# A hybrid decoder layer in fp32r: NSA's q projected first by token tile, 64-column narrow and compressed-score matmuls, and a later chain for the compressed scores

## What is computed

```python
def reference(x, attn_norm_g, w_in, ...):
    h = x
    for l in range(DEPTH):                                   # DEPTH = 1
        a = rms_norm(h, attn_norm_g[l])
        (nq, nkv, ngate, dq, dk, dv, fq, fk, fv, ff, mg) = jnp.split(a @ w_in[l], split_points, axis=-1)
        qa = rms_norm(nq.reshape(B, S, NSA_HEADS, hd), nsa_q_g[l]) * scale
        kv = nkv.reshape(B, S, 3, 2, NSA_GROUPS, hd)
        k_cmp = rms_norm(compress(kv[:, :, 0, 0], ...), nsa_k_g[l, 0])
        v_cmp = compress(kv[:, :, 0, 1], ...)
        ...
        o_a = nsa_attention(qa, k_cmp, v_cmp, k_slc, ..., k_win, ..., ngate..., cmp_end)
        ...                                                  # diff_attention, forgetting_attention
        gates = jax.nn.sigmoid(mg.reshape(B, S, N_BRANCH, D))
        merged = (gates[:, :, 0] * (o_a @ w_br[l, 0]) + gates[:, :, 1] * (o_b @ w_br[l, 1])
                  + gates[:, :, 2] * (o_c @ w_br[l, 2]))
        h = h + merged @ w_o[l]
        h = h + conv_ffn(rms_norm(h, ffn_norm_g[l]), ...)
    return h

# in nsa_attention, for 128 tokens at a time:
dist_c = tpos[:, None] - cmp_end[None, :]
s_c = jnp.einsum('btgrd,bngd->bgrtn', qg, k_cmp)             # 8 heads, 31 compressed keys
s_c = s_c - sl[..., None] * dist_c
p_c = masked_softmax(s_c, dist_c >= 0)
o_c = jnp.einsum('bgrtn,bngd->btgrd', p_c, v_cmp)
```

## Time and profile before

| | us |
|---|---|
| median of 3 runs | 976.08 (975.51 to 976.84) |
| profiled execution, device time | 978.79 |
| its span, first to last instruction | 977.0 |
| PE busy in the span | 958.5 (98%) |
| DVE, ACT, POOL busy | 559.8, 426.2, 209.8 |
| PE's start in the span, first transpose | 8.25 |

### The profile page before, as it was taken

The page is one execution under the profiler, slowest core; times in us unless marked ns, Lnnn a source line. Parts: engine busy times, 40 slices in busy tenths (PEclk is TensorE's granted clock), DMA queues, the critical chain, the costliest instruction groups (busy, mean ns, idle before and its releaser), DMA issues.

```text
span 977.0 us, 12185 instructions
## 1 busy us (share of the span) xinstructions
PE 958.5 (98%) x4625; PEld 794.5 (81%) x4625; DVE 559.8 (57%) x1063; ACT 426.2 (44%) x770; POOL 209.8 (21%) x250
## 2 busy tenths in 40 slices
PE   6999999999999999999999999999999999999998
PEld 5787877788888888888888888888888888888887
DVE  6737787864366895546567454655655665522113
ACT  5335776754256653445777333423222322221110
POOL 3000457640001112212455220121112121100000
PEclk9999999999999999999999999999999999999999
DMA  6512110112222212222211242223222322232222
GB/s 237 219 44 86 45 44 1 43 45 86 87 89 85 87 44 87 86 87 87 81 50 44 87 172 87 87 89 123 91 87 87 121 95 86 87 117 99 87 87 86
DMA packets 13691, 86.33 MB, mean 88 GB/s; under 512 B 1473, under 2 KB 1985, under 8 KB 4289
## 3 DMA queue, kind: packets, MB, share of 16 engines
q1 hardware_dynamic: 13632, 85.55, 24.2%
HBM read 83.44 MB, written 2.10 MB: 88 GB/s over the span
## 4 chain that ended last, share of the span: by engine, by line
PE 89%; DVE 7%; ACT 2%; issue 2%; DMA 0%; SPq 0%; ACTq 0%; DVEq 0%
PE ps L1531 22%; PE ps L1533 22%; PE ps L1532 22%; PE ps L1715 10%; PE ps L1559 4%; PE ps L1672 1%; PE ps L1671 1%; PE ps L1700 1%; DVE prob_n L1232 1%; DVE wl L1013 1%; PE ps L1586 1%; DVE ptn_l L1267 1%; PE ps L1793 1%; PE ps L1795 1%; DVE prob L1232 1%
## 5 line engine op out<-in xcount | busy, mean ns | idle before, releaser
L1013 DVE TENSOR_TENSOR wl<-raw,wh 128x512 fp32r<-128x512 f32 (+2 forms) x118 | 173.5, 1475 | 136.4 <-ACT wh L701 133.8
L701 ACT ACTIVATE wh<-raw 128x2048 fp32r<-128x2048 f32 (+1 forms) x58 | 109.4, 1886 | 157.9 <-PE ps L1533 140.3
L1531 PE MATMUL ps<-aT_h,wh 128*128 128x512 f32 (+1 forms) x376 | 146.7, 390 | 0.8 <-DVE aT_l L1022 0.8
L1532 PE MATMUL ps<-aT_l,wh 128*128 128x512 f32 (+1 forms) x376 | 146.4, 389 | 0.0
L1533 PE MATMUL ps<-aT_h,wl 128*128 128x512 f32 (+1 forms) x376 | 146.4, 389 | 0.0
L1531 PE MATMUL ps<-wh,aT_h 128*128 128x512 f32 x256 | 102.0, 398 | 0.0
L1533 PE MATMUL ps<-wh,aT_l 128*128 128x512 f32 x256 | 100.0, 391 | 0.0
L1532 PE MATMUL ps<-wl,aT_h 128*128 128x512 f32 x256 | 99.8, 390 | 0.0
L1514 POOL TENSOR_TENSOR gl<-gl,rstdT 128x512 f32<-128x512 f32 x22 | 44.5, 2022 | 234.5 <-ACT gl L987 234.5
L1470 POOL TENSOR_SCALAR prob_n<-prob_n,coef 128x384 f32<-128x384 f32 (+3 forms) x64 | 67.7, 1071 | 114.6 <-DVE coef L1249 114.3
L1531 PEld LDWEIGHTS ps<-aT_h,wh 128*128 128x128 f32 (+1 forms) x376 | 70.0, 186 | 16.5 <-issue 1.0
(11 more groups left out here) (250 smaller groups left out, 1796.1 us busy)
## 6 DMA issues: line engine op xcount, KB each, us to landing
raw<-wblk SPq DMA_DIRECT2D x72, 1024.0 KB, 4.7
x<-x SPq DMA_DIRECT2D x4, 512.0 KB, 5.2
w_sb<-w SPq DMA_DIRECT2D x1, 2048.0 KB, 9.2
hid<-x SPq DMA_DIRECT2D x1, 2048.0 KB, 7.7
out<-outt SPq DMA_DIRECT2D x8, 256.0 KB, 2.0
stage<-consts SPq DMA_DIRECT2D x1, 708.5 KB, 4.7
later<-consts SPq DMA_DIRECT2D x1, 448.0 KB, 5.4
par<-params SPq DMA_DIRECT2D x1, 204.5 KB, 8.3
```

The lines of the kernel that those rows point to most:

```text
L701: nc.scalar.activation(wh[b % 2][:, 0:n], raw[b % RING][:, 0:n], ACT.Copy).then_inc(hi_ready, 4)
L1013: ins = nc.vector.tensor_tensor(wl[b % RING][:, cols], raw[b % RING][:, cols], wh[b % 2][:, cols].bitcast(f32), ALU.subtract)
L1531: nc.tensor.matmul(dst, a_h, b_h, start=start, stop=False)
L1532: nc.tensor.matmul(dst, a_h, b_l, start=False, stop=False)
```

## The change

- The block order of NSA becomes `nq`, `small`, `cmp`, `sw`. `nq0` is loaded in four pieces between the tiles of `x`; a row `grow` of the norm's gains is loaded too.
- The gain goes onto `x` ahead of the transpose: two matmuls spread `grow` over 128 partitions into two PSUM banks, and DVE's scaling multiplies by the row factor and by that bank. A transposed tile (four chunks of one token tile, a half of the channels) is taken by ACT and DVE tile by tile. Eight transposes of the identity run on PE ahead of all.
- `first_tiles` projects `nq0` for token tiles 0 to 3 as each is ready, then `nq1`; the next tile's transposes stand between a tile's sixth and seventh matmul.
- `small` holds the high and the low weights side by side as 64 stationary columns: 16 matmuls for 24. `ST` adds the two halves with a stacked identity `id2`.
- The steps after the projections are in another order: the DVE and ACT work of the `nq` chunks and of `gate0`'s block stands ahead of `compression(1)` and `(2)`, and PE's `compression(0)`, `(1)`, `(2)` stand later.
- `SC` is 8 matmuls of 64 columns (high and low keys side by side) with no distance matmul. DVE adds the distance and the two halves, then takes minimum and subtracts (`SCV`); POOL multiplies by the slopes (`SCM`) and, after `CN`, by the coefficients (`CNM`); ACT's exponential is `SCA`.
- In the table `SC` stands at 4 and `TC` at 12, the steps between at 5, 6, 7, 8, 9; `OC` for both groups at 15. `SC` and `ON(i, 0)` use bank 2, `TC` and `ON(i, 1)` bank 3. `ON(i, 0)` is opened by `VA`.

```diff
-PROJ = {NSA: ["cmp", "small", "nq", "sw"], DIFF: ["dq", "dk", "dv"], FOX: ["fq", "fk", "fv"]}
+PROJ = {NSA: ["nq", "small", "cmp", "sw"], DIFF: ["dq", "dk", "dv"], FOX: ["fq", "fk", "fv"]}
...
-            put(per * i + 3, "SC", i)
-            put(per * i + 5, "CN", i)
-            put(per * i + 7, "TC", i)
+
+            put(per * i + 4, "SC", i)
...
+            put(per * i + 12, "TC", i)
...
+            sp.dma_start(x0[:, 0, :], xv[0]).then_inc(x_in[0], 16)
+            sp.dma_start(grow[:, :].rearrange("o (p c) -> o p c", c=KD), params[:, C_ROW:C_ROW + KD].rearrange("(o p) c -> o p c", o=1)).then_inc(grow_in, 16)
+            first(0)
+            first(1)
+            sp.dma_start(x0[:, 1, :], xv[1]).then_inc(x_in[1], 16)
...
+            def x_scale(n):
+
+                half, t = divmod(n, TT)
+                dve.wait_ge(rstd_ready, t + 1)
+                dve.wait_ge(gain_rows, half + 1)
+                cols = slice(half * S, half * S + S)
+                nc.vector.scalar_tensor_tensor(xn0[:, t, cols], x0[:, t, cols], rstd[:, t:t + 1], ps[6 + half][:, :], ALU.mult, ALU.mult).then_inc(xn_ready, 1)
...
+            x_sum(0)
+            x_scale(0)
+            split(0, 0)
+            x_lo(0)
+            split(0, 1)
+            x_sum(1)
+            x_scale(1)
+            split(0, 2)
+            split(0, 3)
+            x_lo(1)
+            x_sum(2)
+            x_scale(2)
+            x_lo(2)
...
-                    split(BI[(m, "sw1")])
-                    compression(1)
                     dve.wait_ge(gain_ready, 1)
                     post_t(m, "nq", (0, 1))
+                    post_t(m, "nq", (2, 3))
+                    split(BI[(m, "gate0")])
+                    compression(1)
                     compression(2)
...
-                        nc.tensor.matmul(bk[:, 0:256], identr[:, :], biasC[:, j].rearrange("p h n -> p (h n)"), start=True, stop=False)
                         for h in range(8):
-                            dst = bk[:, 32 * h:32 * h + 32]
-                            nc.tensor.matmul(dst, q_hl[:, h, rows], kc_hh[:, h // 4], start=False, stop=False)
-                            ins = nc.tensor.matmul(dst, q_hl[:, h, rows], kc_l[:, h // 4, h % 2], start=False, stop=h == 7)
+                            ins = nc.tensor.matmul(bk[:, 64 * h:64 * h + 64], q_hl[:, h, rows], kc_hl[:, h // 4, h % 2].rearrange("p a n -> p (a n)"),
+                                                   start=True, stop=True)
```

More of the change, by code:

```diff
@@ L110, with opens @@
 HEAD_FILL = {NSA: 24, DIFF: 4, FOX: 4}
+def opens(n):
+    q, kb = STEPS[n]
+    kind, g, i, blocks = group_of(q)
+    return kind == "slc" and g == 0 and kb == 0
 def has_pv(m, q):
@@ L473, in build @@
         sel = small("sel", [P, 8], f32r)
+        id2 = small("id2", [64, 32])
         kss = small("kss", [HD, 1])
@@ L570, in bank, with small_w @@
             return ps[place[key][0]]
-        hi_order = [("N", 0, k) for k in range(KD)]
+        PIECED = [BI[(NSA, "nq0")], BI[(NSA, "nq1")], BI[(NSA, "cmp")]]
+        SMALL = BI[(NSA, "small")]
+        def small_w():
+            return wh[SMALL % 2][:, 0:KD * 64].rearrange("p (k r c) -> p k r c", r=2, c=32)
+        hi_order = [("N", 0, n) for n in range(2 * TT)]
         for m in (NSA, DIFF, FOX):
@@ L649, in _, with first @@
             sp.dma_start(ident[:, :], consts[:, K_ID:K_ID + P]).then_inc(id_in, 16)
-            for t in range(TT):
+            def first(piece):
+                cols = slice(piece * 512, piece * 512 + 512)
+                sp.dma_start(raw[0][:, cols], wblk[0, :, cols]).then_inc(first_in[piece], 16)
+            sp.dma_start(x0[:, 0, :], xv[0]).then_inc(x_in[0], 16)
[3 more added lines that the diff above has]
+            sp.dma_start(x0[:, 1, :], xv[1]).then_inc(x_in[1], 16)
+            first(2)
+            first(3)
+            for t in (2, 3):
                 sp.dma_start(x0[:, t, :], xv[t]).then_inc(x_in[t], 16)
@@ L1606, in _ @@
             pe.wait_ge(id_in, 16)
[L1607 to L1614 removed]
+            for n in range(8):
+                nc.tensor.transpose(ps[5][:, 0:P], ident[:, :], ident[:, :])
@@ new lines, in _, with x_transposes @@
+            pe.wait_ge(ones_set, 1)
+            pe.wait_ge(grow_in, 16)
+            for half in range(2):
+                nc.tensor.matmul(ps[6 + half][:, :], ones1[:, :], grow[:, half * S:half * S + S], start=True, stop=True).then_inc(gain_rows, 1)
+            def x_transposes(n):
+                if n < 2 * TT:
+                    half, t = divmod(n, TT)
+                    pe.wait_ge(xn_ready, n + 1)
+                    transposes(("N", 0, n), [xn0[:, t, k * P:(k + 1) * P] for k in range(4 * half, 4 * half + 4)])
@@ L1616, in _ @@
+            x_transposes(0)
             for m in (NSA, DIFF, FOX):
@@ L1927, in pack_params @@
     parts = [cols(a["attn_norm_g"][0]), cols(a["ffn_norm_g"][0]), conv, cols(a["conv_b"][0]), cols(a["diff_subln_g"][0])]
-    out = np.concatenate(parts + [twice(g) for g in gains] + pe + rows, axis=1)
-    assert out.shape == (P, C_END)
+    out = np.concatenate(parts + [twice(g) for g in gains] + pe + rows + [a["attn_norm_g"][0].reshape(P, KD)], axis=1)
+    assert out.shape == (P, C_ROW + KD)
     return np.ascontiguousarray(out)
```

335 lines of the change are left out of this document (217 added, 118 removed).

## The result

| kernel | us, median of the runs | against before |
|---|---|---|
| before, beside it | 975.99 (975.51 to 976.84) | |
| changed | 997.27 (996.78 to 999.94) | 1.0223 (1.0203 to 1.0242) |

The account below looks back on a forecast made before the run. PE, busy nearly all the time, was taken to bound the kernel. The terms summed to +6.0 us on the profiled span of 977.0, giving 983.0; less 0.9 the forecast was 982.0 us, range 973.5 to 989.

Parts of the forecast that it names:

- q by token tile: Head: with q projected first, each tile waits for the one before; q ends at 44.4 instead of 37.3, +7.1 us.
- the tile chain: Head, rival, 18%: DVE and ACT keep PE's 3.2 us per tile, so the 7.1 falls to 0; 973.
- small: Narrow projection ahead of the attention: 16 matmuls for 24, -1.8 us, its weight work hidden.
- KCT: Compression, ahead of the attention: PE waits for ktok behind ACT's and DVE's queued work, +4.1 us (3 to 4.5).
- Tile 0 and first scores: Before NSA's first scores: tile 0's compressed chain later against PE, +3.3 us (1.5 to 4.5), then +0.8 for the scores.
- The 0.8: First scores of NSA: they wait for k_ll as ACT stood still behind POOL, +0.8 us (0 to 1.5).
- The attention phase: From NSA's first scores on: TC and SC in later slots -2.6, clock -3.4, ACT waiting for POOL +2.0 us.
- `SC` of three tiles: Compressed scores: 8 matmuls for 17 save 0.96 us per tile; the prediction had -3.8 for all four tiles.
- waits gone: Attention phase: TC five slots and SC one slot later remove PE's waits of 2.0 and 0.6 us, -2.6.
- -3.4 (clock): Attention phase: two half-clock stretches of 3.4 us stay away with shorter SC blocks and no wait, -3.4 us (0 to -3.4).
- ACT behind POOL: NSA attention: exponential waits for POOL, +2.0 us (0.7 per tile); rival, 12%: 2 us more per tile, 986 to 989.
- low-clock rival: Head, rival, 17%: PE stays at 1.2 GHz until 30 us, q ends at 48.8, +4.4 us: 986.5.

Follow-up runs that it names:

- scm_kct: scm_early with the compression's norm (kss to ktok) ahead of the split of gate0 on ACT and DVE; 984.23 us.
- warm_fill: scm_kct with twelve more identity transposes on PE in tile 0, after two of its twelve matmuls, their result unread; 982.78 us.
- small64: The kernel before with one edit: the narrow projection small as 64 columns, 16 matmuls for 24; 977.62 us, ratio 1.0000.
- scm_early: The changed kernel with POOL's slope multiplication of tiles 1 to 3 one slot earlier, ahead of the pair of probability scalings; 988.94 us.
- attn_scm: The kernel before with only the attention part of the change, and POOL's slope multiplication one slot earlier; 973.98 us, ratio 0.9958.
- pool_off: The changed kernel with the two multiplications of the compressed chain (slope and coefficient) on DVE again; 991.15 us.
- best1: attn_oc with small at 64 columns, 16 matmuls instead of 24; 974.19 us.
- attn_oc: attn_scm with the two compressed-value matmuls of tiles 1 to 3 one and two slots later; 974.21 us.

## Why the prediction was wrong, step by step

- **q by token tile: right.** 44.9 for 44.4. The takings of `aT_l` by DVE come 4.3 us apart in the first half (18.31, 22.60, 26.89; 4.45 was worked out) and 3.6 in the second. The clock rose at 19.2 us (a 512-column matmul takes 0.43 before and 0.23 after), against 13.8 in the kernel before, so not until 30; and the tile chain did not hide. What the low clock costs here is small: in `scm_kct`, where it rose at 16.7, q ends 0.4 us earlier (44.55), in `warm_fill` 1.5 (43.45).
- **`small`: 3.69 us, as worked out,** but a gain on PE of 1.8 is 0.3 by the first scores when nothing else moves (`small64`: 87.12 us from first projection to first scores for 87.39). In `small64` the cover that the term took for granted is not there (0.69 of wait for q's weights). In the changed kernel no wait follows `small`. In both, the doubled transposes, 0.6 us, were left out of the sum.
- **KCT: the wait right (3.97 for 4.1), its price short by 1.6.** After it, F ran at half clock (3.96 us for 2.32). The sum charged waits at their length only.
- **Tile 0 and first scores: the number near, partly by luck.** The 3.3 came as 1.3 (`nrm`) and 1.8 (`TC`), 3.1. But the releaser is not POOL's `pc`, as the prediction said:

```profile
112.36 0.60 PE L1943 MATMUL ps<-ident,pc 128*64 128x128 f32 x4 [1.81 <-ACT gate L968]
```

`pc` is done at 111.49. ACT's `gate`, which stands behind the exponential, a weight split and a 1.28 us load of its function table, ends at 112.22 and frees the bank of `TC`. No term had that wait. The 0.8 did not come (0.43 of wait, as before). The compressed block was as short as worked out: 0.81 us from its first of 8 matmuls (104.02) to the one behind them (104.83). With the terms above, the first score matmul was due 12.8 us later by the sum and came 14.4 later.
- **The attention phase is the step that failed.** The sum had -2.9 (`SC` of three tiles), -2.6 (waits gone), -3.4 (clock) and +2.0 (ACT behind POOL) = -6.9; the phase from NSA's first scores to DIFF's grew by 4.2. The failing step is "ACT behind POOL": I took 0.7 us per tile, with 0 to 2 as bounds, and ACT waited 2.2 to 2.7 at each. With the order put right and nothing else (`scm_early`) the phase is 9.3 us shorter, 196.7 for 206.0: that is what the term stood for, where the sum had 2.0. The chain was named in the text (POOL's pairs of 0.95 to 1.25, ACT's exponential, the scores behind ACT), and not followed in order: `coef` is made by DVE directly behind the compressed block, so that POOL's pair comes first although the slope is ready earlier, which the order of the two queues shows without any time. Nor did it stop at ACT: a wait of ACT came back to DVE and PE longer than it was (2.17, 2.72, 3.24), since DVE's and PE's next work needs what ACT does after it. And the waits took the clock with them, so that the 3.4 us of gain turned into a loss: three half-clock stretches in the phase, where the profile of before has two. PE alone, in the changed kernel, behind the waits that end at 93.66, 147.39, 176.38 and 204.79:

```profile
93.83:97.72 3.89, 3.89 (x10) 0.57 0.00 0
148.95:151.90 2.95, 2.95 (x10) 0.50 0.92 322
176.40:179.60 3.20, 3.20 (x10) 0.50 0.00 0
206.60:210.40 3.80, 3.25 (x10) 0.55 0.01 4
```

- **Had POOL's order been right, the sign holds and the size does not.** In `attn_scm` the stretch of scores takes 91.03 us for 96.31 in the trace of before, 5.3 less, clock at 1.00 throughout. Without the term for ACT the sum had 8.9, and 2.0 of the 5.3 is the clock of one execution (next section). A second term failed here: PE's 2.0 and 0.6 us of waits went, as summed, but 4.0 us of others came. In `scm_early` those for `nmx`, `ptn_l` and `pcT` are 3.0, 1.8 and 1.4, where before had 0.8, 1.4 and none. The prediction named DVE as late next and left its waits as they were.
- **The whole miss.** The span was to be 983.0 and is 995.6: 12.6 us, of which 11.1 are the attention phase (+4.2 for -6.9) and 1.6 the way to the first scores. The time is 15.3 us off; the other 2.7 are the conversion, since 0.9 was taken from the span where a run takes 1.8 more.
- **Slips in the sums, none of which matters.** By its own working q ends at 44.5, tile 0's terms add to 3.45, and the low-clock rival stands at 986.4, where 44.4, 3.3 and 986.5 were taken. The transposes of before are 0.213 and 0.109 us apart, so 4.7 and 9.2 per us, where 5.3 and 10 were counted.
- **The rival that came true** was "ACT behind POOL", given 12%, and at 986 to 989 its price was 8 us too low. The mechanism was right; its size was taken from inside bounds that no row had set.

## What to carry to other kernels

An operation that is handed to another engine is priced by what stands ahead of it in that engine's queue, and what that waits for; walk the two queues in order at one tile before putting a number to it. Here one slot in the table of events was worth 8.3 us, more than the 5.6 us of all the matmuls that the change saved. A long wait of PE is to be charged with the half-clock stretch behind it: all eight waits of 3 us or more in these traces have one, 3.4 us long and so worth about 1.7 us, and in `scm_early` and `pool_off` one of 6.8 us stands behind KCT. Short waits do not rule it out: before's second stretch, from 177.7, has no wait over 0.4 us in the 7 us ahead of it. And a saving on PE counts only up to the next semaphore that is not ready: two edits that took 1.8 and 3.8 us of matmuls from PE moved the median by less than 0.1% each.

## What the runs showed of the hardware

**Before has more than one time.** Its 41 runs beside the experiments lie at 975.3 to 976.1 where the mean granted clock is 1.000 (one at 977.5), and at 978.1 to 979.2 where it is 0.996 or 0.997, with those at 0.998 between (976.3 to 978.3). The profiled execution, 978.79 at 0.996, was one of the latter; it holds two half-clock stretches, the first of which is in the earlier trace rows. `small64`, whose attention phase is that of before, was profiled with none, and its scores take 2.0 us less than in the profile of before (busy time by stretch):

```profile
102.14:196.43 94.29, 88.53 (x505) 72.22 (x506) 77.38 (x271) 69.95 (x187) 62.24 (x60) 1.00 0.10 35
```

So the -3.4 for the clock was counted on a profile with two such stretches, while the four runs beside the result (975.5 to 976.8) lie where before has one such stretch or none; subtracting 0.9 from the span (every run takes 1.8 more than its span) hid it. Of the 41 later runs 14 are at 1.000, 7 at 0.998 and 20 below. Whether such a stretch falls is not fixed by the program: what makes one execution take it and the next not stays open. `attn_scm`, `best1` and `attn_oc` had 0.999 or 1.000 in all their 19 runs. That they wait less is not the reason: PE idles 6.4 us in the scores of `attn_scm` and 5.0 in those of before.
